# A decoder layer in one kernel: values times output weights ahead of the attention product, which becomes three passes, and the last expert's down weights split one turn earlier

## The chip, the cores and the metric

The kernel runs on one core of one Trainium2 chip. The metric is the device time of one execution in microseconds (us). Engines are named as in the profile: PE is TensorE (matrix products), PEld its weight loads, DVE is VectorE, ACT is ScalarE, POOL is GpSimd, SP is SyncE, which here only issues DMAs.

## The reference

One decoder layer over 1024 tokens of width 1024, all float32: a mixing stage (gated recurrence beside a state-space model, with an output product), then cross-attention into 256 memory tokens, then a mixture of 32 experts with the top 4 for each token, and a final norm. What the change touches:

```python
q = (xn @ xa_wq).reshape(bsz, s, XA_HEADS, XA_HD)            # 4 heads of 256
kv = (rmsnorm(mem, mem_g) @ xa_wkv).reshape(bsz, m, 2, XA_HEADS, XA_HD)
k, v = kv[:, :, 0], kv[:, :, 1]
scores = jnp.einsum('bshd,bmhd->bhsm', q, k) * (XA_HD ** -0.5)
p = jax.nn.softmax(scores, axis=-1)
o = jnp.einsum('bhsm,bmhd->bshd', p, v).reshape(bsz, s, D_MODEL)
return o @ xa_wo
...
gu = xb @ w_gu + b_gu                                          # each expert, on its tokens
h = (u + 1.0) * (g * jax.nn.sigmoid(SWIGLU_ALPHA * g))       # g, u clamped halves of gu
return h @ w_down + b_down
```

## The kernel before

Each engine has its own program, written out by hand; semaphores order them. PSUM has eight banks, and in everything ahead of the experts a list `order` of units sets which bank a unit gets (its number modulo 8): `begin(u)` makes PE wait until the unit eight places earlier has been read out, `end(u)` tells the others that the bank is filled. The order of `order` is therefore PE's order of work.

**Attention.** `q` (in the tensor YT) and the keys (KT) and values (VV, written as units `vv`) are there. A unit `sc` is the scores of 128 tokens against 256 memory tokens for two heads: four float32 products of 256 columns. DVE takes the maxima (`maxima`, L1731), ACT the exponentials with their sums (L1256), DVE divides (`normalise`, L1737 and L1440), and PE transposes the result in a unit `pt` five steps (`LEAD`) after its scores (L846); ACT copies it to PT (L1246). There are 16 of each. Then 16 units `ot` multiply the values with PT, two float32 products of 512 columns each (L856), and ACT copies them to YT (L1052). Then for each of eight row tiles two units `wo2` (`out_tile`, L863) multiply the result with the output weights, eight float32 products each. DVE adds them to H (L1751), PE transposes the new rows (`xt3`) and multiplies them with the router's weights (`rl`, L881), and DVE picks the top 4 (`top`), while DMAs carry the rows out for the experts.

**Two ways to multiply.** A float32 product shows as two records of PE. Where a product is made in three passes (`passes`, L785; the query product L825; all of the experts), ACT rounds an operand to a shorter form (fp32r, the high part), DVE subtracts it from the original (the low part), and PE adds high x high, low x high and high x low; each such product is one record.

**Experts.** A loop of at most 64 turns in groups of four runs over items, of one tile of 128 tokens or two tiles (up to 192) of one expert; a group is skipped once no item is live, and here 36 items are. In turn i PE makes gate and up of item i (L959, L963), then the down product of item i-1 (L980, L987), and the transposes of the next tokens and of the hidden rows (L1012). SP loads raw weights, ACT makes their high parts (`gate_up_high`, `down_high` L1325, `next_high` L1341) and DVE the low parts (L1890, into WL). The last item's down product thus falls into a turn without an item of its own: there `down_pair` on ACT and `down_low` on DVE split its four parts. Tests such as `by_tiles(act, n_i, first)` are branches that each engine runs for itself in every turn. After the loop the tail adds y_acc (L591 loads it) to a bias product (L1036, L1040), normalises and stores. ACT's first work there is L1420.

## Time and profile before

| | |
|---|---|
| median of 3 runs (lowest to highest) | 2292.22 us (2286.15 to 2293.78) |
| the profiled execution: its time, its span | 2293.89 us, 2292.2 us |
| PE busy | 2187.8 us, 95% of the span |
| DVE busy, ACT busy | 1599.9 us (70%), 1271.1 us (55%) |
| moved by DMA | 555.95 MB, mean 243 GB/s |
| mean granted TensorE clock | 0.977 of full speed |

The profile is of one execution. Times of rows count from the start of its span. A row of the timeline merges like instructions in a row (x48 is 48 of them); what stands in brackets behind it is the idle time before it on its engine, and what ended that. PE's records overlap a little, so the step from one row to the next is a better duration than the row's own length.

### The profile page before, as it was taken

The numbers are of one execution on the slowest core, as the hardware profiler recorded it, in microseconds if no ns is written. First come the engines' busy times: TensorE is split into PE (matmuls) and PEld (weight loads), VectorE is DVE, ScalarE is ACT, GpSimd is POOL, SyncE is SP. The second block draws the span as 40 slices with busy tenths as digits, with TensorE's granted clock in tenths as the row PEclk, the third lists the DMA queues.
The fourth block names the chain that finished last, engine by engine and source line by source line (L and its number), as shares of the span: only waits on it lengthen the run. The fifth ranks groups of instructions, "written<-read, shape, count | busy, mean of one in ns | idle before, by whom it ended". The sixth has DMA issues, their size and how long they took to land.

```text
span 2292.2 us, 32993 instructions
## 1 busy us (share of the span) xinstructions
PE 2187.8 (95%) x9450; PEld 1663.6 (73%) x9451; DVE 1599.9 (70%) x1540; ACT 1271.1 (55%) x1209; POOL 459.4 (20%) x357
## 2 busy tenths in 40 slices
PE   7999999999998699999999999999999999999986
PEld 4455668887454588887887888788878887888873
DVE  5645842404134889887779977997889779997773
ACT  3136241415213477666667756776677667776663
POOL 0791000000000113122213212221322123132210
PEclk9999999999998799999999999999999999999997
DMA  5103331111123499989799979999899799997984
GB/s 171 37 1 112 111 146 38 37 37 37 58 96 134 165 378 384 343 305 324 259 320 375 375 275 338 356 361 337 320 316 376 274 323 374 378 379 272 322 294 161
DMA packets 233715, 555.95 MB, mean 243 GB/s; under 512 B 19972, under 2 KB 20200, under 8 KB 232200
## 3 DMA queue, kind: packets, MB, share of 16 engines
q1 hardware_dynamic: 218448, 512.41, 61.0%
q0 software_dynamic: 13264, 42.63, 7.5%
q10 hardware_dynamic: 1960, 0.35, 0.1%
q8 instruction: 26, 0.43, 0.1%
q14 instruction: 17, 0.14, 0.0%
HBM read 518.38 MB, written 33.69 MB: 241 GB/s over the span
## 4 chain that ended last, share of the span: by engine, by line
PE 82%; DVE 7%; issue 6%; ACT 3%; DVEq 1%; ACTq 1%; DMA 0%
PE PS L959 22%; PE PS L627 20%; PE PS L963 12%; PE PS L980 9%; PE PS L987 5%; PE PS L785 4%; PE PS L825 4%; DVE WL L1890 3%; PE PS L951 2%; PE PS L1012 1%; PE PS L917 1%; PE PS L645 1%; PE PS L1040 1%; ACT WH L1320 1%; ACT WH L1325 1%
## 5 line engine op out<-in xcount | busy, mean ns | idle before, releaser
L1890 DVE TENSOR_TENSOR WL<-WA,WH 128x2048 fp32r<-128x2048 f32 x288 | 651.6, 2285 | 70.3 <-ACT WH L1341 46.6
L1890 DVE TENSOR_TENSOR WL<-H,WH 128x2048 fp32r<-128x2048 f32 x144 | 329.2, 2286 | 82.5 <-ACT WH L1320 60.2
L959 PE MATMUL PS<-WH,XEH 128*128 128x512 f32 x1344 | 362.9, 392 | 0.0
L963 PE MATMUL PS<-WL,XEH 128*128 128x512 f32 x1344 | 352.5, 390 | 0.0
L1341 ACT CAST WH<-WA 128x2048 fp32r<-128x2048 f32 x140 | 267.3, 1910 | 144.7 <-PE PS L987 143.2
L959 PE MATMUL PS<-WH,XEL 128*128 128x512 f32 x1152 | 311.5, 393 | 0.0
L963 PEld LDWEIGHTS PS<-WL,XEH 128*128 128x128 f32 x1344 | 253.6, 189 | 53.2
L959 PEld LDWEIGHTS PS<-WH,XEH 128*128 128x128 f32 x1344 | 254.0, 189 | 51.4
L959 PEld LDWEIGHTS PS<-WH,XEL 128*128 128x128 f32 x1152 | 218.6, 190 | 46.4
L980 PE MATMUL PS<-WH,HTH 128*128 128x512 f32 x672 | 187.9, 401 | 6.3 <-DVE WL L1890 6.3
L1320 ACT CAST WH<-H 128x2048 fp32r<-128x2048 f32 x72 | 136.9, 1909 | 86.8 <-PE PS L963 86.6
L1325 ACT CAST WH<-WA 128x2048 fp32r<-128x2048 f32 x72 | 137.5, 1911 | 76.5 <-PE PS L963 75.8
L987 PE MATMUL PS<-WL,HTH 128*128 128x512 f32 x672 | 176.8, 391 | 0.0
L2182 POOL CAST SELR<-WA 128x128 fp32r x35 | 31.0, 885 | 713.1 <-PE PS L917 713.1
L1320 ACT CAST WH<-WA 128x2048 fp32r<-128x2048 f32 x72 | 136.7, 1908 | 36.6 <-PE PS L963 36.6
L1325 ACT CAST WH<-H 128x2048 fp32r<-128x2048 f32 x72 | 136.6, 1907 | 35.1 <-PE PS L963 33.1
L980 PE MATMUL PS<-WH,HTL 128*128 128x512 f32 x576 | 155.4, 392 | 0.0
L987 PEld LDWEIGHTS PS<-WL,HTH 128*128 128x128 f32 x672 | 126.7, 189 | 26.8
L980 PEld LDWEIGHTS PS<-WH,HTH 128*128 128x128 f32 x672 | 121.8, 190 | 28.3 <-DVE WL L1890 6.5
L627 PE MATMUL PS<-XT,WB 128*128 128x512 f32 (+1 forms) x384 | 138.5, 521 | 1.6 <-DVE XT L1464 1.6
L2198 POOL DMA_INDIRECT y_acc<-WA x42 | 90.9, 2164 | 245.2 <-ACT WA L1393 156.1
L980 PEld LDWEIGHTS PS<-WH,HTL 128*128 128x128 f32 x576 | 108.7, 189 | 23.9
(322 smaller groups left out, 2891.2 us busy)
## 6 DMA issues: line engine op xcount, KB each, us to landing
WA<-in_exp_w_gu SPq DMA_DIRECT2D x216, 1024.0 KB, 7.6
H<-in_exp_w_gu SPq DMA_DIRECT2D x72, 1024.0 KB, 7.0
WA<-in_exp_w_down SPq DMA_DIRECT2D x72, 1024.0 KB, 9.5
H<-in_exp_w_down SPq DMA_DIRECT2D x72, 1024.0 KB, 8.3
WB<-in_xa_wkv SPq DMA_DIRECT2D x4, 2048.0 KB, 8.4
WB<-in_w_in SPq DMA_DIRECT2D x3, 2048.0 KB, 9.6
y_acc<-H SPq DMA_DIRECT2D x9, 512.0 KB, 2.6
H<-in_x SPq DMA_DIRECT2D x4, 1024.0 KB, 5.9
```

What stands on the lines that cost most here:

```text
L627: return nc.tensor.matmul(o, a, b, start=(k == 0), stop=(k == n - 1))
L785: ins = nc.tensor.matmul(o, x(k), w(k), start=k_first and n == 0, stop=k_last and n == 3 * len(ks) - 1)
L825: ins = nc.tensor.matmul(o, w[:, k, j * P:(j + 1) * P], x[:, :, k, :], start=n == 0, stop=n == 3 * K - 1)
L959: nc.tensor.matmul(PS[:, 2 * h + t, :], x[:, KT4 * half + k, t * P:(t + 1) * P], WH[:, j % 4, k * HALF:(k + 1) * HALF], start=False, stop= ...
L963: ins = nc.tensor.matmul(PS[:, 2 * h + t, :], XEH[:, KT4 * half + k, t * P:(t + 1) * P], WL[:, j % 4, k * HALF:(k + 1) * HALF], start=Fals ...
L980: nc.tensor.matmul(PS[:, 4 + 2 * t + c, :], hx[:, 2 * m + k, t * P:(t + 1) * P], WH[:, m, k * D + c * HALF:k * D + (c + 1) * HALF], start= ...
L987: ins = nc.tensor.matmul(PS[:, 4 + 2 * t + c, :], HTH[:, 2 * m + k, t * P:(t + 1) * P], WL[:, m, k * D + c * HALF:k * D + (c + 1) * HALF], ...
L1320: nc.scalar.copy(WH[:, s, :], raw_gu(4 + s)).then_inc(gu_high, 1)
L1325: nc.scalar.copy(WH[:, m, :], raw_dn(m)).then_inc(dn_high, 1)
L1341: nc.scalar.copy(WH[:, s, :], raw_gu(s)).then_inc(gu_high, 1)
L1890: v.tensor_tensor(WL[:, s, :], src, WH[:, s, :].bitcast(F32), sub).then_inc(done, 1)
L2198: g.indirect_dma_start(out=y_acc[:, :], out_offset=bass.IndirectOffsetOnAxis(ap=IDS[0:n, t, 0:1], axis=0), in_=YS[0:n, t, :], in_offset=No ...
```

## The change

Two rewrites at once. In attention, `vv` becomes `vt` (the values transposed), and 16 units `vw` multiply each head's values with that head's rows of the output weights, among the score steps; `ot` is gone. `sc` now runs over the first two heads of all tiles, then the other two. ACT rounds `pt` and `vw` to their high parts (`high`), DVE subtracts (`low_part`), and `out_tile` makes 24 products in three passes. In the experts, ACT's and DVE's branches on the number of tiles are merged (`down_pair`, `gate(1)` and `hidden(1)` move into `first`), and the last item's down weights are split in its own turn (`last_high`, `last_low`). The loads of y_acc are cut into 1, 1, 3 and 3 row tiles where they were 2 each.

```diff
-        VV = wa(10240, MT, D)
+        VT = wa(10240, K, ML)
         KV = WA[:, 8192:12288]
-        PP = wa(0, 4, 2, ML)
-        PT = XT[:, :, :].rearrange("p k t -> p (k t)").rearrange("p (h m t) -> p h m t", h=NH, m=MT)
+        PP = wa(12288, 4, 2, ML)
+        PTL = XTR[:, :].rearrange("p (k l s) -> p l k s", l=L, k=K)
+        PTH = WAR[:, 0:8192].rearrange("p (l k s) -> p l k s", l=L, k=K)
...
-        att = [(l, hp) for l in range(L) for hp in range(2)]
-        LEAD = 5
-        for n in range(len(att) + LEAD):
+        att = [(l, hp) for hp in range(2) for l in range(L)]
+        vws = [(c, h, m) for c in range(2) for h in range(NH) for m in range(MT)]
+        LEAD = 4
+        steps_at = []
+        for n in range(L + len(vws)):
             if n < len(att):
-                order.append(("sc",) + att[n])
-            if n >= LEAD:
-                order.append(("pt",) + att[n - LEAD])
-        order += [("ot", h, d, f) for h in range(NH) for d in range(2) for f in range(2)]
+                steps_at.append(("sc",) + att[n])
+            if LEAD <= n < len(att) + LEAD:
+                steps_at.append(("pt",) + att[n - LEAD])
+            if n >= L:
+                steps_at.append(("vw",) + vws[n - L])
+        order += steps_at
+        high_after = [[] for _ in att]
+        for n in range(L + len(vws)):
+            here = high_after[min(n, len(att) - 1)]
+            if LEAD <= n < len(att) + LEAD:
+                here.append(("pt",) + att[n - LEAD])
+            if n >= L and (n - L) % MT == MT - 1:
+                here += [("vw",) + vws[n - L - 1], ("vw",) + vws[n - L]]
+        high_no = {u: n + 1 for n, u in enumerate(sum(high_after, []))}
         for n in range(L + 1):
             order += [("wo2", 0, n)] * (n < L)
...
-                        for n in range(4):
-                            sp.dma_start(ACC[:, 2 * n:2 * n + 2, :],
-                                         y_acc[0:T, :].rearrange("(p l) d -> p l d", l=L)[:, 2 * n:2 * n + 2, :]) \
+                        for n, (l0, l1) in enumerate(acc_part):
+                            sp.dma_start(ACC[:, l0:l1, :],
+                                         y_acc[0:T, :].rearrange("(p l) d -> p l d", l=L)[:, l0:l1, :]) \
                                 .then_inc(acc_in[n], 16)
...
-            for n in range(len(att) + LEAD):
-                if n < len(att):
-                    l, hp = att[n]
-                    o = begin(("sc", l, hp))
+            w_o2 = []
+            for kind, *u in steps_at:
+                o = begin((kind, *u))
+                if kind == "sc":
+                    l, hp = u
...
-                    end(("sc", l, hp), ins)
-                if n >= LEAD:
-                    l, hp = att[n - LEAD]
-                    pe.wait_ge(pn_done, n - LEAD + 1)
-                    o = begin(("pt", l, hp))
+                elif kind == "pt":
+                    n = att.index(tuple(u))
+                    pe.wait_ge(pn_done, n + 1)
...
                         for m in range(MT):
                             ins = nc.tensor.transpose(o[:, (2 * hh + m) * P:(2 * hh + m + 1) * P],
-                                                      PP[:, (n - LEAD) % 4, hh, m * P:(m + 1) * P], ident[:])
-                    end(("pt", l, hp), ins)
-            units_read(pe, "pt")
-            for h in range(NH):
-                for d in range(2):
-                    for f in range(2):
-                        o = begin(("ot", h, d, f))
+                                                      PP[:, n % 4, hh, m * P:(m + 1) * P], ident[:])
+                else:
+                    c, h, m = u
+                    if h == 0 and m == 0:
+                        w_o2.append(weights(("o2", c)))
+                    for d in range(2):
+                        ins = mm(o, VT[:, 2 * h + d, m * P:(m + 1) * P], w_o2[c][:, 2 * h + d, :], d, 2)
+                end((kind, *u), ins)
+            def out_tile(c, n):
+                for hp in range(2):
+                    unit_read(pe, ("pt", n, hp))
+                if n == 0:
+                    for h in range(NH):
                         for m in range(MT):
-                            c = h * HD + d * P
-                            ins = mm(o, VV[:, m, c:c + P], PT[:, h, m, f * HALF:(f + 1) * HALF], m, MT)
-                        end(("ot", h, d, f), ins)
-            units_read(pe, "ot")
-            w_o2 = [weights(("o2", c)) for c in range(2)]
-            def out_tile(c, n):
+                            unit_read(pe, ("vw", c, h, m))
                 o = begin(("wo2", c, n))
-                for k in range(K):
-                    ins = mm(o, YT[:, k, n * P:(n + 1) * P], w_o2[c][:, k, :], k, K)
+                w = WBR[:, chunk_no[("o2", c)] % 2, :, :]
+                i = 0
+                for p_t, m_v in ((PTH[:, n], w), (PTL[:, n], w), (PTH[:, n], MVL[:, c])):
+                    for k in range(K):
+                        ins = mm(o, p_t[:, k, :], m_v[:, k, :], i, 3 * K)
+                        i += 1
                 end(("wo2", c, n), ins)
...
-            def keep(n):
-                l, hp = att[n]
-                u = ("pt", l, hp)
+            def high(u):
                 wait_filled(act, u)
-                evac(act, nc.scalar.copy(PT[:, 2 * hp:2 * hp + 2, :, l * P:(l + 1) * P],
-                                         bank(u).rearrange("p (h m t) -> p h m t", h=2, m=MT)), u)
+                if u[0] == "pt":
+                    _, l, hp = u
+                    o = PTH[:, l, 4 * hp:4 * hp + 4, :]
+                    nc.scalar.copy(o, bank(u).rearrange("p (k s) -> p k s", k=4)).then_inc(att_high, 1)
+                else:
+                    _, c, h, m = u
+                    wait_filled(act, ("vw", c, h, MT - 1))
+                    nc.scalar.copy(WBR[:, chunk_no[("o2", c)] % 2, 2 * h + m, :], bank(u)).then_inc(att_high, 1)
...
-                if n >= LEAD:
-                    keep(n - LEAD)
-            for n in range(len(att) - LEAD, len(att)):
-                keep(n)
-            for h in range(NH):
-                for d in range(2):
-                    for f in range(2):
-                        copy_unit(("ot", h, d, f), YT[:, 2 * h + d, f * HALF:(f + 1) * HALF])
+                for u in high_after[n]:
+                    high(u)
...
                 def down_pair(m0):
                     with act.If_cmp(n_p, 0, "IS_GT"):
-                        with act.If_cmp(n_i, 0, "IS_GT"):
-                            for m in (m0, m0 + 1):
-                                act.wait_ge(gu_used, 8 * i + m + 9)
-                                down_high(m)
-                        with act.Else():
-                            down_high(m0)
-                            down_high(m0 + 1)
+                        for m in (m0, m0 + 1):
+                            act.wait_ge(gu_used, 8 * i + m + 9)
+                            down_high(m)
+
+                def last_high(m):
+                    act.wait_ge(rd_in[m], 16 * i + 16)
+                    act.wait_ge(gu_used, 8 * i + m + 9)
+                    act.wait_ge(dn_used, 4 * i + m + 5)
+                    nc.scalar.copy(WH[:, m, :], raw_dn(m)).then_inc(dn_high, 1)
...
+                    down_pair(0)
+                    gate(1, tiles)
+                    down_pair(2)
+                    if tiles == 2:
+                        upper_up(1)
...
-                by_tiles(act, n_i, first)
-                down_pair(0)
-                by_tiles(act, n_i, lambda tiles: gate(1, tiles))
-                down_pair(2)
-                with act.If_cmp(n_i, P, "IS_GT"):
-                    upper_up(1)
-                counts.fetch(i)
-                by_tiles(act, n_n, next_tokens(0))
-                with act.If_cmp(n_n, 0, "IS_GT"):
+                def tokens_and_weights(tiles):
+                    next_tokens(0)(tiles)
                     next_high(0)
                     next_high(1)
-                by_tiles(act, n_n, next_tokens(1))
+                    next_tokens(1)(tiles)
+
+                def last_weights(m0):
+                    with act.If_cmp(n_i, 0, "IS_GT"):
+                        last_high(m0)
+                        last_high(m0 + 1)
+
+                by_tiles(act, n_i, first)
+                counts.fetch(i)
+                by_tiles(act, n_n, tokens_and_weights, lambda: last_weights(0))
                 by_tiles(act, n_i, hidden(0))
                 with act.If_cmp(n_n, 0, "IS_GT"):
                     next_high(2)
                     next_high(3)
+                with act.Else():
+                    last_weights(2)
                 by_tiles(act, n_i, hidden(1))
                 by_tiles(act, n_p, keep_y)
...
 
+            def low_part(u):
+                dve.wait_ge(att_high, high_no[u])
+                if u[0] == "pt":
+                    _, l, hp = u
+                    ks = slice(4 * hp, 4 * hp + 4)
+                    evac(dve, v.tensor_tensor(PTL[:, l, ks, :], bank(u).rearrange("p (k s) -> p k s", k=4),
+                                              PTH[:, l, ks, :].bitcast(F32), sub), u)
+                else:
+                    _, c, h, m = u
+                    hi = WBR[:, chunk_no[("o2", c)] % 2, 2 * h + m, :].bitcast(F32)
+                    evac(dve, v.tensor_tensor(MVL[:, c, 2 * h + m, :], bank(u), hi, sub), u)
+
             for n in range(len(att) + 1):
                 if n < len(att):
                     maxima(n)
                 if n > 0:
                     normalise(n - 1)
+                    for u in high_after[n - 1]:
+                        low_part(u)
...
+                    with dve.If_cmp(n_p, 0, "IS_GT"):
+                        down_low(0)
+                    gate_min(1, tiles)
+                    with dve.If_cmp(n_p, 0, "IS_GT"):
+                        down_low(1)
+                        down_low(2)
+                    hidden(1, tiles)
+
+                def last_low(m0):
+                    with dve.If_cmp(n_i, 0, "IS_GT"):
+                        for m in (m0, m0 + 1):
+                            dve.wait_ge(dn_high, 4 * i + m + 5)
+                            low_weights(m, raw_dn(m), dn_low)
...
-                with dve.If_cmp(n_p, 0, "IS_GT"):
-                    down_low(0)
-                by_tiles(dve, n_i, lambda tiles: gate_min(1, tiles))
-                with dve.If_cmp(n_p, 0, "IS_GT"):
-                    down_low(1)
-                    down_low(2)
-                by_tiles(dve, n_i, lambda tiles: hidden(1, tiles))
                 counts.fetch(i)
                 by_tiles(dve, n_n, next_tokens(0), lambda: dve.sem_inc(xel_done, 1))
                 with dve.If_cmp(n_p, 0, "IS_GT"):
-                    down_low(3)
-                with dve.If_cmp(n_n, 0, "IS_GT"):
+                    with dve.If_cmp(n_i, 0, "IS_GT"):
+                        down_low(3)
+
+                def weights_and_tokens(tiles):
                     gate_up_low(8)
                     gate_up_low(9)
-                by_tiles(dve, n_n, next_tokens(1), lambda: dve.sem_inc(xel_done, 1))
+                    next_tokens(1)(tiles)
+
+                def no_tokens():
+                    last_low(0)
+                    dve.sem_inc(xel_done, 1)
+
+                by_tiles(dve, n_n, weights_and_tokens, no_tokens)
                 by_tiles(dve, n_i, low_hidden(0))
                 with dve.If_cmp(n_n, 0, "IS_GT"):
                     gate_up_low(10)
                     gate_up_low(11)
+                with dve.Else():
+                    last_low(2)
                 by_tiles(dve, n_i, low_hidden(1))
```

How the instructions move. On PE, the end of attention; L627 is `mm` (L643 in the changed kernel), L846 (L861) are the transposes of `pt`, and products out of XT and WA are `ot`, out of WB and YT `wo2`. Before:

```order
L627 MATMUL PS<-WA,YT 128x256 x4
L846 MATMUL PS<-ident,WA 128x128 x4
L627 MATMUL PS<-WA,YT 128x256 x4
L846 MATMUL PS<-ident,WA 128x128 x24
L627 MATMUL PS<-XT,WA 128x512 x32
L627 MATMUL PS<-WB,YT 128x512 x24
L645 MATMUL PS<-ident,H 128x128 x8
L627 MATMUL PS<-WB,YT 128x512 x8
```

In the changed kernel, at the same place (products out of WB and WA are `vw`; those out of WBR or YTR with WAR or XTR are the three passes of `wo2`):

```order
L861 MATMUL PS<-ident,WA 128x128 x4
L643 MATMUL PS<-WB,WA 128x512 x2
L861 MATMUL PS<-ident,WA 128x128 x4
L643 MATMUL PS<-WB,WA 128x512 x10
L643 MATMUL PS<-WBR,WAR 128x512 x8
L643 MATMUL PS<-WBR,XTR 128x512 x8
L643 MATMUL PS<-YTR,WAR 128x512 x8
```

The block of 32 products has become pairs between the transposes and scores, and a `wo2` unit of eight products has become three times eight.

On DVE, one step of attention: the maxima, their scaling, the reciprocal and the division. Before:

```order
L1731 TENSOR_REDUCE sm<-PS 128x2
L1443 TENSOR_SCALAR sm<-sm 128x2
L1737 RECIPROCAL sm<-sm 128x2
L1440 TENSOR_TENSOR WA<-WA,sm 128x512
L1731 TENSOR_REDUCE sm<-PS 128x2
```

In the changed kernel, a step in the second half of the scores:

```order
L1761 TENSOR_REDUCE sm<-PS 128x2
L1473 TENSOR_SCALAR sm<-sm 128x2
L1767 RECIPROCAL sm<-sm 128x2
L1470 TENSOR_TENSOR WA<-WA,sm 128x512
L1775 TENSOR_TENSOR XTR<-PS,WAR 128x4x128
L1780 TENSOR_TENSOR YTR<-PS,WBR 128x512 x2
L1761 TENSOR_REDUCE sm<-PS 128x2
```

One subtraction for `pt` and, in every other step, two for `vw` have come behind the division.

On ACT, the last part of a turn of the expert loop, from the branch for the other parts of the weights (L1413 before) to the copy of the hidden rows' second half. Before:

```order
L1413 COMPARE_AND_BRANCH
L1338 ISA
L1339 ISA
L1340 ISA
L1341 CAST WH<-WA 128x2048
L1339 REGISTER_ALU
L1340 REGISTER_ALU
L1341 CAST WH<-WA 128x2048
L1413 UNCONDITIONAL_BRANCH
L431 COMPARE_AND_BRANCH
```

In the changed kernel, what has come between that part (which ends with the first row) and the hidden rows:

```order
L1441 UNCONDITIONAL_BRANCH
L1433 COMPARE_AND_BRANCH
L1353 ISA
L1354 ISA
L1355 ISA
L1356 CAST WH<-H 128x2048
L1354 REGISTER_ALU
L1355 REGISTER_ALU
L1356 CAST WH<-H 128x2048
L1433 UNCONDITIONAL_BRANCH
L447 COMPARE_AND_BRANCH
```

The two casts of the last item's down weights stand ahead of `hidden(1)` on ACT.

## Rows read from the trace of the kernel before

**Rows 1.** The page: the chain that ended last, by engine and by line

```profile
PE 82%; DVE 7%; issue 6%; ACT 3%; DVEq 1%; ACTq 1%; DMA 0%
PE PS L959 22%; PE PS L627 20%; PE PS L963 12%; PE PS L980 9%; PE PS L987 5%; PE PS L785 4%; PE PS L825 4%; DVE WL L1890 3%; PE PS L951 2%; PE PS L1012 1%; PE PS L917 1%; PE PS L645 1%; PE PS L1040 1%; ACT WH L1320 1%; ACT WH L1325 1%
```

**Rows 2.** Stretch of the loop: length, busy PE, PEld, DVE, ACT, POOL, clock, DMA share, GB/s

```profile
800.00:2190.00 1390.00, 1369.44 (x6272) 1124.45 (x6272) 1173.31 (x838) 954.98 (x718) 328.14 (x219) 1.00 0.95 336
```

**Rows 3.** Timeline of PE, attention to the first output tiles: start, length, line

```profile
525.09 10.60 PE L627 MATMUL PS<-WA,YT 128*128 128x256 f32 x48 [0.93 <-issue]
...
551.12 1.89 PE L627 MATMUL PS<-WA,YT 128*128 128x256 f32 x8
...
553.29 1.89 PE L627 MATMUL PS<-WA,YT 128*128 128x256 f32 x8
...
564.35 29.40 PE L627 MATMUL PS<-XT,WA 128*128 128x512 f32 x64 [1.71 <-ACT XT L1246]
...
594.69 20.84 PE L627 MATMUL PS<-WB,YT 128*128 128x512 f32 x48 [0.93 <-issue]
```

**Rows 4.** Stretches of the scores, of `ot`, and of `wo2`: columns as in rows 2

```profile
525.00:563.00 38.00, 35.31 (x192) 30.78 (x192) 28.53 (x65) 28.08 (x80) 0.00 (x0) 1.00 0.16 56
563.00:594.00 31.00, 29.40 (x64) 12.67 (x64) 0.00 (x0) 10.04 (x19) 0.00 (x0) 0.94 0.00 1
...
637.00:728.00 91.00, 91.00 (x319) 48.67 (x317) 24.23 (x62) 14.11 (x28) 0.00 (x0) 1.00 0.33 116
```

**Rows 5.** The subtraction of a low part out of PSUM, ns min/median/max

```profile
L1686 DVE TENSOR_TENSOR WAR<-PS,XTR x10: 691/692/693, 432.4 to 440.0; 128x512 fp32r<-128x512 f32 x10
```

**Rows 6.** The chain in order of time: query product; two turns of wo2

```profile
435.61 88.55 PE PS L825 x384
...
637.89 15.52 PE PS L627 x48
654.29 15.52 PE PS L627 x48
```

**Rows 7.** Timeline of PE, keys (256 columns) and values (512 columns)

```profile
237.04 27.86 PE L627 MATMUL PS<-XT,WB 128*128 128x256 f32 x128 [1.64 <-DVE XT L1464]
264.74 27.63 PE L627 MATMUL PS<-WB,XT 128*128 128x512 f32 x64
```

**Rows 8.** Timeline of PE at the router's first product

```profile
624.73 2.45 PE L627 MATMUL PS<-WA,XT 128*128 128x32 f32 x16 [1.46 <-DVE WA L1440]
626.99 10.03 PE L627 MATMUL PS<-WB,YT 128*128 128x512 f32 x16
```

**Rows 9.** Timeline of all engines, end of the last item and last down product

```profile
2220.20 2.29 DVE L1890 TENSOR_TENSOR WL<-H,WH 128x2048 fp32r<-128x2048 f32 x1 [0.33 <-issue]
...
2227.91 0.60 PE L1012 MATMUL PS<-ident,WA 128*128 128x128 f32 x4
...
2234.79 2.07 PE L980 MATMUL PS<-WH,HTH 128*128 128x512 f32 x4 [6.29 <-DVE WL L1890]
...
2248.85 1.11 ACT L1393 ACTIVATE WA<-PS,WA 128x1024 f32<-128x1024 f32 x1 [11.03 <-PE PS L987]
```

**Rows 10.** Down weights' loads (L540) after 2200 us: us from issue to landing

```profile
DMA to landing us min/median/max: 4.8/5.1/7.6
```

**Rows 11.** The chain after the last product: ACT's queue in its empty turns

```profile
2249.98 0.04 ACTq L1404
...
2252.78 0.04 ACTq L1404
...
2253.10 0.96 ACTq L452
...
2256.58 0.28 ACTq L452
...
2261.69 1.05 ACT HTH L1420
```

**Rows 12.** PE's longest wait in the expert loop: us, times, longest

```profile
PE PS L1012 <- DVE XEL L1886: 13.7, 13, 4.7
```

30 lines of the change are left out of this document (17 added, 13 removed).

## The prediction

> **What bounds the kernel now.** The page's chain first: PE has 82% of what ended last, the expert products alone nearly half [rows 1]. The stretches confirm it for the expert loop: from 800 to 2190 us PE is busy 1369.4 of 1390 us at full clock, while the DMA engines are busy at 0.95 and DVE at 1173 [rows 2]. So what the change does inside a normal turn of the loop can give back 20.6 us at most, and only a saving of PE work, or of a wait of PE, counts elsewhere. Next the timeline of PE in attention: one step (a score unit and a transpose unit) takes 553.29 - 551.12 = 2.17 us with no idle time, then `ot` starts after a wait of 1.71 for ACT, and the first `wo2` after another 0.93 [rows 3]. Attention, too, is bound by PE, with small waits where one kind of unit ends. The end is different: ahead of the last down product PE waits 6.29 us for the low parts of the weights [rows 9], and from ACT's copy of its result at 2248.85 [rows 9] ACT's queue runs through empty turns until its first work of the tail at 2261.69 [rows 11].
>
> **Values.** `vv` takes 27.63 us of PE (64 records of 512 columns), `kk` 27.86 (128 of 256) [rows 7]. `vt` has the shape and count of `kk`, so it costs +0.2 us at most. The loads behind it wait for its middle and its end, as they did. I take 0.
>
> **Attention.** Removed: 16 `ot` units, and the two waits around them. Added to the score steps: 16 `vw` units of the same shape, two products of 512 columns, four records. A record of 512 columns takes 20.84 / 48 = 0.43 us, so a unit 1.72 [rows 3]. PE's work is then 16 x 2.17 + 16 x 1.72 = 62.2 us, where the stage took 594.69 - 525.09 = 69.6 us [rows 3]: 7.4 us less, if nothing new makes PE wait. What hides beside it: ACT copied each `pt` and each `ot` and rounds each `pt` and `vw` now, 32 of one size as before: 28.08 + 10.04 = 38 us [rows 4]. DVE was busy 28.53 us for 16 steps [rows 4], 1.8 a step, 1.9 with gaps, and gets 32 subtractions of 0.69 [rows 5]: 16 x 1.9 + 32 x 0.69 = 52.5 us. Both are below 62.2. In the dense part, steps 8 to 15, PE needs 3.9 us a step, DVE 1.9 + 2 x 0.69 = 3.3. The wait added on DVE is for ACT's high part; behind it stand the next maxima, then ACT's exponentials, then a `pt` that PE makes four steps later, so there is room. Tightest are the banks: the first `vw` of a pair is only read out once the second is made and rounded, and PE wants its bank eight units later. From the start of a step DVE has it out after 1.7 (scores) + 1.9 (own work) + 2 x 0.69 = 5.0 us, and PE comes to it after 3.9 + 1.7 = 5.6. That fits by 0.6. If it did not, four pairs would each lose about 1 us. Bounds: 2 to 8 us gained; I take 7.4.
>
> **Output product.** Each of 16 `wo2` units was 8 float32 products, 16 records x 0.43 = 6.9 us. It becomes 24 products in three passes. The query product has their shape: 384 of them in 88.55 us, 0.2306 each [rows 6], so 5.53 us. Saved: 16 x 1.37 = 22 us (22.5 by 20.84 / 48 unrounded). The rest of a row tile's turn of 654.29 - 637.89 = 16.4 us (transposes, router) stays [rows 6]. DVE has 24.23 of 91 us in this stage and ACT 14.11 [rows 4], 4.4 and 2.5 a turn, so they don't take over at 13.6. The wait of 1.46 us for the scaled router weights, and the slow products after it (10.03 us for 16 records against 6.9) [rows 8], come again: it hangs on DVE's add and multiply behind the second tile's product, whatever that took. Bounds: 18 (the slow piece grows, or a turn gets a wait of 0.5) to 23; I take 22.
>
> By the rows a float32 product takes 0.86 us and one pass of the other kind 0.2306, a ratio of 3.7 [rows 3, 6]. The Trainium skill, "FP8 and Floating Point Precision", TensorE Precision Notes, has a true FP32 product at 4 passes through the array. By that, a unit would fall by a quarter of 6.9, to 5.2, and the stage by 27 us; the sum goes by the rows.
>
> **The normal turns.** DVE's and ACT's order of work is the same, with fewer branches. PE's longest wait there, 13.7 us in 13 pieces for the low part of the next tokens [rows 12], comes at the end of a run of DVE work without gaps, so branches hardly lengthen it. 0, bounds -4 (slower) to +4.
>
> **The last item.** Now its weights' split stands ahead of the last down product, on queues that run in order. The last load is issued when DVE ends `down_low(3)`, about 2220.20 + 2.29 = 2222.5 [rows 9], and lands after about 5.1 [rows 10], 2227.7. ACT may write a part once PE has used the old one; counted back from 2227.91 [rows 9] in parts of 12 products of 0.23 with one block of transposes between, that is from 2219.5, 2222.2, 2225.4 and 2228.1, the last one to 2230. `hidden(0)` stands ahead of the third, and only after the fourth comes `hidden(1)`. DVE: five subtractions of 2.29 (`down_low(3)` and four) and two of 0.69 from 2220.2 make 12.8, so 2233.1 with PE's signal. PE starts the last down product at 2233.2 in place of 2234.79: the wait of 6.29 shrinks by 1.6 only, since the last low part of the hidden rows now comes after the weights. With a last load of 7.6 [rows 10] the start is 2235.7, 0.9 late. The transposes of the second half wait for parts 0 and 1 on DVE (2227.1), PE comes at 2227.91: covered by 0.8.
>
> **The empty turns.** A turn without work costs ACT 2252.78 - 2249.98 = 2.8 us [rows 11] for 12 tests, 0.23 a test. Eight tests are left, and three such turns follow: 3 x 4 x 0.2 = 2.4. PE leaves the loop by turns of its own, which stay as they were, and is next late; I let 2.2 count. The smaller first loads of y_acc end no wait, since PE wasn't waiting for them. Together the end gives 3.8 us; bounds -1 to 8 (8 if the clock also stays up over the shorter wait).
>
> **Sum.** 7.4 + 22 + 0 + 3.8 = 33 us off the profiled execution's 2293.89: 2261. The median of the runs, 2292.22, is 1.7 lower, so the same saving gives 2259. I say 2260.
>
> **Rivals.**
> 1. As summed: 2260, own range 2254 to 2267. Chance 0.65.
> 2. DVE or the banks hold attention back. For it: a margin of 0.6 us a pair, and DVE loaded to 85%. Against: the counts above. At 1 to 1.5 us for each of four pairs, and 1 to 2 at the hand-over to `wo2`, 6 us are lost: 2266. Chance 0.13.
> 3. The end gains nothing: the order of ACT's queue makes `hidden(1)` late and a slow load eats the rest; the empty turns hit a slow one like the 0.96 against 0.28 of the loop's own read [rows 11]. 4 to 5 us lost: 2264. Chance 0.12.
> 4. Turned over: the longer branch bodies on ACT and DVE cost a jump that has to load code in each turn. For it: that row of 0.96 [rows 11] is a stumble of 0.7 us after a jump back, and the two-tile case now stands as a longer block ahead of the one-tile case. Against: PE is busy 98.5% through 36 items [rows 2], so such stumbles are hidden now. It decides from 33 / 36 = 0.9 us a turn that PE feels; at 1.3 us, 47 are lost: 2306. Chance 0.04. The Trainium skill, "Runtime: NRT & Kernel Launch", Instruction fetch mechanics, says that a taken branch out of the loaded window makes the sequencer fetch the target before it goes on; the 0.7 us would fit, but no row here shows what the longer bodies do.
> 5. More than summed (the clock stays up at the wait before the last product and at the router, the loop gains 4): 2251. Chance 0.06.
>
> **Numbers.** Cases 1, 2, 3 and 5 lie between 2248 and 2272; cut to 8 in 10 the range is 2252 to 2271. About 0.3% (7 us) is what a measurement can tell here. Faster by more than that holds in all but case 4 and its milder form, in which the turns eat about all: 0.95 faster, 0.02 within, 0.03 slower.
>
> **What would show it.** In the changed profile: no `ot` records; PE from the first score to the first `wo2` in 62 to 64 us; a `wo2` unit at 5.5, a row tile's turn at 13.6 to 13.8; PE's wait before the last down product 4.5 to 5 us, ended by DVE's low part of the hidden rows; ACT's empty turns near 2.0; the stretch of the loop still at 98% PE. Wrong would be: a wait of PE on a bank or on DVE among the `vw` units; a turn above 14 us; a lower granted clock from the first `vw` to the router; a longer wait for the next tokens in normal turns.

## The result and the profile after

| | before | changed |
|---|---|---|
| median (lowest to highest, 3 runs each) | 2292.22 us (2286.15 to 2293.78) | 2254.76 us (2253.54 to 2256.15) |
| profiled execution: time, span | 2293.89, 2292.2 us | 2254.76, 2253.0 us |
| PE busy, share of the span | 2187.8 us, 95% | 2156.8 us, 96% |
| mean granted TensorE clock | 0.977 | 0.983 |

The ratio is 0.9842, with a 95% interval of 0.9824 to 0.9861: 37.5 us faster, where 32 (2292 to 2260) were forecast, inside the range of 2252 to 2271. The kernel before ran 65 times in all (median 2289.97 us, 2286.04 to 2294.55), most of them near 2286.5 or near 2293; the median of the three above and both of its profiles are of the upper group, so some 2 of the 37.5 us are the draw. The chain of the changed kernel answers to [rows 1]. PE is still what ended last in four fifths of the span; the page says:

```profile
PE 80%; issue 8%; DVE 6%; ACT 3%; DVEq 1%; ACTq 1%; DMA 1%; SPq 0%
```

Next the timeline of PE from the first score to the router, as [rows 3, 8]:

```profile
525.58 8.87 PE L643 MATMUL PS<-WA,YT 128*128 128x256 f32 x40 [0.98 <-ACT YT L1072]
...
543.39 1.88 PE L643 MATMUL PS<-WB,WA 128*128 128x512 f32 x4
545.11 1.89 PE L643 MATMUL PS<-WA,YT 128*128 128x256 f32 x8
546.83 0.60 PE L861 MATMUL PS<-ident,WA 128*128 128x128 f32 x4
547.27 1.88 PE L643 MATMUL PS<-WB,WA 128*128 128x512 f32 x4
...
579.19 8.75 PE L643 MATMUL PS<-WB,WA 128*128 128x512 f32 x20
587.37 2.42 PE L643 MATMUL PS<-WBR,WAR 128*128 128x512 f32 x8
...
612.47 1.97 PE L643 MATMUL PS<-WA,XT 128*128 128x32 f32 x16 [1.46 <-DVE WA L1470]
614.28 2.10 PE L643 MATMUL PS<-WBR,WAR 128*128 128x512 f32 x8
...
628.03 2.11 PE L643 MATMUL PS<-WBR,WAR 128*128 128x512 f32 x8
```

A dense step is 547.27 - 543.39 = 3.88 us, with no idle time in any row of the units `vw`, and the waits of 1.71 and 0.93 [rows 3] at the change of units are gone. At the router PE waits 1.46 us, as in [rows 8], but what follows runs at full speed: eight products in 616.22 - 614.28 = 1.94 us, where in the kernel before the 16 records of the unit took 10.03 and those of the next one 7.03. A row tile's turn is 628.03 - 614.28 = 13.75 us, where it was 16.4 [rows 6].

The end, in the timelines of PE, ACT and DVE, as [rows 9, 11]:

```profile
2194.19 0.60 PE L1032 MATMUL PS<-ident,WA 128*128 128x128 f32 x4
2194.39 1.90 ACT L1356 CAST WH<-H 128x2048 fp32r<-128x2048 f32 x1 [0.81 <-PE PS L1007]
2196.19 0.58 ACT L1406 CAST HTH<-PS 128x512 fp32r<-128x512 f32 x1
2196.32 2.29 DVE L1934 TENSOR_TENSOR WL<-H,WH 128x2048 fp32r<-128x2048 f32 x1 [0.37 <-ACT WH L1356]
2196.67 1.12 ACT L1419 ACTIVATE WA<-PS,WA 128x1024 f32<-128x1024 f32 x1
2198.53 0.68 DVE L2034 TENSOR_TENSOR HTL<-PS,HTH 128x512 fp32r<-128x512 f32 x1
2199.35 1.46 PE L1000 MATMUL PS<-WH,HTH 128*128 128x512 f32 x4 [4.57 <-DVE HTL L2034]
...
2212.32 1.11 ACT L1419 ACTIVATE WA<-PS,WA 128x1024 f32<-128x1024 f32 x1 [14.53 <-PE PS L1007]
2223.80 1.04 ACT L1450 CAST HTH<-H 96x1024 fp32r<-96x1024 f32 x1 [10.36 <-issue]
```

PE's wait fell from 6.29 to 4.57 us and is now ended by the low part of the hidden rows, behind the last subtraction of the weights.

Cut at the same landmarks, the two profiled executions differ stage by stage. The landmarks on PE are the first score, the first `wo2`, the last transposes of rows for the router, the last transposes (L1012, now L1032) of the first turn and of the last item, the last down product and the last product of the tail; on ACT its last `keep_y` copy and its first work of the tail. Three of before's were not shown yet:

```profile
728.28 1.07 PE L645 MATMUL PS<-ident,H 128*128 128x128 f32 x8
...
800.43 1.11 PE L1012 MATMUL PS<-ident,WA 128*128 128x128 f32 x4 [4.74 <-DVE XEL L1886]
...
2284.12 1.88 PE L1040 MATMUL PS<-WA,ident 128*128 128x512 f32 x4
```

and in the changed kernel they stand at:

```profile
696.83 1.07 PE L661 MATMUL PS<-ident,H 128*128 128x128 f32 x8
...
768.63 1.12 PE L1032 MATMUL PS<-ident,WA 128*128 128x128 f32 x4 [4.77 <-DVE XEL L1930]
...
2245.01 1.88 PE L1060 MATMUL PS<-WA,ident 128*128 128x512 f32 x4
```

| stage (us) | before | changed | difference | forecast |
|---|---|---|---|---|
| up to the first score | 525.09 | 525.58 | +0.5 | 0 |
| attention | 69.60 | 61.79 | -7.8 | -7.4 |
| output products, router | 133.59 | 109.46 | -24.1 | -22 |
| item lists, first turn | 72.15 | 71.80 | -0.35 | 0 |
| loop up to the last item's transposes | 1427.48 | 1425.56 | -1.9 | 0 |
| to the last down product | 6.88 | 5.16 | -1.7 | -1.6 |
| to ACT's copy of it | 14.06 | 12.97 | -1.1 | 0 |
| empty turns, to ACT's tail | 12.84 | 11.48 | -1.4 | -2.2 |
| tail's sums, and from there to the end | 30.5 | 29.2 | -1.3 | 0 |
| sum | | | -39.2 | -33 |

### The profile page after: what moved, and what is told of

Same layout as the page of the kernel before. It is cut to its first block, busy times and chain, and to the rows that moved or that the text cites. A ratio compares the mean times of both kernels' runs of the same rounds, so it can differ in the third digit from the quotient of the medians.

```text
span 2253.0 us, 32880 instructions
## 1 busy us (share of the span) xinstructions
PE 2156.8 (96%) x9642; PEld 1696.1 (75%) x9643; DVE 1620.0 (72%) x1572; ACT 1271.3 (56%) x1213; POOL 453.0 (20%) x357
## 4 chain that ended last, share of the span: by engine, by line
PE 80%; issue 8%; DVE 6%; ACT 3%; DVEq 1%; ACTq 1%; DMA 1%; SPq 0%
PE PS L979 21%; PE PS L643 20%; PE PS L983 11%; PE PS L1000 9%; PE PS L1007 5%; PE PS L801 4%; PE PS L841 4%; DVE WL L1934 2%; PE PS L971 2%; PE PS L1032 1%; ACT WH L1339 1%; PE PS L937 1%; PE PS L661 1%; PE PS L1060 1%; ACT WH L1362 1%
## 5 line engine op out<-in xcount | busy, mean ns | idle before, releaser
L643 PE MATMUL PS<-XT,WB 128*128 128x512 f32 (+1 forms) x512 | 166.2, 486 | 1.6 <-DVE XT L1494 1.6
L1344 ACT CAST WH<-H 128x2048 fp32r<-128x2048 f32 x70 | 132.9, 1907 | 33.5 <-PE PS L983 32.0
L643 PEld LDWEIGHTS PS<-XT,WB 128*128 128x128 f32 x512 | 97.2, 190 | 69.1 <-issue 62.6
```

The lines of the kernel that those rows point to most:

```text
L643: return nc.tensor.matmul(o, a, b, start=(k == 0), stop=(k == n - 1))
L1344: nc.scalar.copy(WH[:, m, :], raw_dn(m)).then_inc(dn_high, 1)
```

## The experiments

Each kernel ran beside the kernel before on the same chip; ratios are to that, with 95% intervals. The stages named are those of the table.

### One part alone

**e_att: the attention part on top of the kernel before.** The edit is the upper part of the diff, from VT to `low_part`.

> The kernel before with the values-times-weights rewrite alone. If the parts simply add on PE's path: attention stage 61.8 us from the first score to the first output product, a row tile's turn 13.76 us, the router's transposes 31 to 32 us earlier than before, and 2258 to 2262 us in all. If the gain of the loop's stretch (1.9 us in the two profiles) belongs to the attention part (other starting times of loads), the first expert's last transposes to the last item's come 1.9 us closer and the time is 2257 to 2259. Rival, part of the 37 us comes only from both together: above 2263.

Measured: 2263.41 us, ratio 0.9884 (0.9866 to 0.9903). The expected 2258 to 2262 us were missed by 1.4. Attention takes 61.79 us and the output stage 109.46, to 0.01 us as in the changed kernel. So these two stages don't need the loop part. The 8.7 us that this profile has more than the changed one lie behind it: loop 1428.42 (+2.9), to the last down product 6.98 (+1.8), to ACT's copy 14.23 (+1.3), empty turns 13.40 (+1.9), tail (+1.1). The rival's bound of 2263 was passed by 0.4 us. It was no good test, since it left out both the loop part's own gain and the pieces at a lower clock that are told under before_again; so the whole times leave the rival open (see e_loop).

**e_loop: the loop part on top of the kernel before**, from `acc_part` and `last_high` on.

> The kernel before with the rewrite of the expert loop's end alone (with the y_acc loads of 1, 1, 3 and 3 row tiles). If the parts add: 4 to 8 us faster than before, 2284 to 2288, with PE's wait ahead of the last down product 4.5 to 4.7 us in place of 6.29 and 11.5 us from ACT's copy of the last result to its first work of the tail in place of 12.84. If the branches help the normal turns, the loop's stretch is 1.5 to 2 us shorter here too. Rival, longer branch bodies cost in each turn: slower than before.

Measured: 2286.35 us (12 runs, 2282.08 to 2290.57) beside 2287.66 (17 runs, 2286.04 to 2294.03), ratio 0.9993 (0.9982 to 1.0003): by the medians not told apart, lowest and highest run 4.0 and 3.5 us lower. The stages show the parts that were expected: to the last down product 5.20 (wait 4.61), empty turns 11.60. Rival 4, a price in each turn, would be 47 us and is refuted. The whole times don't add up: beside the same 17 executions of the kernel before, e_att saves 24.3 us, e_loop 1.3, and both parts (e_acc, below) 33.5. By the profiles e_loop is 8.5 us shorter (span 2283.7 for 2292.2). Where the missing 8 us come from is not shown: 10 of those 17 executions took 2286.0 to 2288.0 us, and no profile of such a one was taken.

**e_acc: y_acc loaded by two row tiles, as before.**

```diff
-        acc_part = ((0, 1), (1, 2), (2, 5), (5, L))
...
+                pe.wait_ge(acc_in[l // 2], 16)
```

> The changed kernel with the y_acc loads of two row tiles each, as before. If PE never waits for them: the same time within 1 us (2255). Rival, the small first loads are what lets the tail's first products start earlier (they start 1.3 us closer to ACT's first work of the tail than before): 1 to 1.5 us slower, with a wait of PE in the tail ended by a load.

Measured: 2254.15 us, ratio 0.9848 (0.9833 to 0.9863), no wait of PE on a load in the tail. The smaller loads are worth nothing here, as forecast.

**e_merge: merged branches, but the last item's weights split one turn later.**

```diff
+                def late_high():
+                    with act.If_cmp(n_p, 0, "IS_GT"):
+                        for m in range(4):
+                            down_high(m)
-                by_tiles(act, n_i, first)
+                by_tiles(act, n_i, first, late_high)
...
-                by_tiles(act, n_n, tokens_and_weights, lambda: last_weights(0))
+                by_tiles(act, n_n, tokens_and_weights)
```

(likewise `late_low` on DVE, in place of `last_low`.)

> The changed kernel with the last item's down weights split in the turn behind it, as before; attention, the merged branches and the y_acc loads stay. If the merged branches alone make the normal turns shorter: 1424 to 1425.6 us from the first item's last transposes to the last item's, as in the changed kernel, where the kernel with the attention part alone has 1428.4; and if the split alone makes the end's wait shorter: PE waits 6.3 us ahead of the last down product again, and 1.7 to 2 us are lost against the changed kernel (2256.5). Rival, the loop's 3 us hang on the split or on when the loop starts: the loop's stretch is 1427 to 1428.5 here as well, and 4 to 5 us are lost.

Measured: 2260.61 us, ratio 0.9876 (0.9854 to 0.9898): 5.9 us above the changed kernel's 2254.76. PE's wait is 6.18 us again, ended by the low part of the weights: the split is what shortened it. But the loop is 1428.43 us, the rival's number, and neither theory explains it. Its PE row at the start of an item, and the same one in the changed kernel:

```profile
878.32 0.49 PE L971 MATMUL PS<-BIASR,SELR 128*128 128x512 f32 x1 [0.56 <-issue]
```

```profile
878.64 0.49 PE L971 MATMUL PS<-BIASR,SELR 128*128 128x512 f32 x1 [0.38 <-issue]
```

PE's own program is the same in both, and what it waits for here the profile doesn't show. In about twenty places of the 35 turns, most of them the start of an item, it comes 0.1 to 0.2 us later, 3.5 us in all with the low-clock pieces of the next section taken off. The edit touches branches on ACT and DVE alone, and it is not a test more in a turn: ACT has one else branch more and two fewer, DVE one more and one fewer. So PE feels how the branches of the other engines lie, in spite of its 98.5%. Whether it is the longer body that is jumped over, its place in the code or its order is not shown.

### Where the loop's difference comes from

**before_again: the kernel before once more.**

> The kernel before, unchanged, as a second profile of it. Its 17 runs beside the last experiments lay in two groups, around 2286.5 and around 2293. If this profile falls in the lower group: its loop from the first item's last transposes to the last item's is near 1424 us in place of 1427.5, or the slow piece at the router is shorter, or both, and so the change's saving over a like execution is 32 to 33 us rather than 37. If the profile lies in the upper group, its stages repeat those of the first one within 1 us.

Measured: 2292.44 us (12 runs), profiled execution 2292.01, again of the upper group, so the expectation for the lower one (a saving of 32 to 33 us) stays untested. Up to ACT's tail every stage of the table is within 0.05 us of the first profile (attention 69.60, output 133.60, loop 1427.46, to the down product 6.88), except the stretch ahead of the first score (1.9 us less). A profile is a good ruler, then. What differs between kernels are short pieces behind a wait of PE in which the granted clock falls to one half (of its two levels, the lower). PE in e_att, timeline:

```profile
1430.58 0.49 PE L970 MATMUL PS<-BIASR,SELR 128*128 128x512 f32 x1 [0.67 <-issue]
1430.92 1.31 PE L978 MATMUL PS<-WH,XEH 128*128 128x512 f32 x4
1432.02 1.91 PE L978 MATMUL PS<-WH,XEL 128*128 128x512 f32 x4
1433.73 1.69 PE L982 MATMUL PS<-WL,XEH 128*128 128x512 f32 x4
```

and in the changed kernel, at the same item and behind the same wait:

```profile
1430.42 0.49 PE L971 MATMUL PS<-BIASR,SELR 128*128 128x512 f32 x1 [0.63 <-issue]
1430.75 1.08 PE L979 MATMUL PS<-WH,XEH 128*128 128x512 f32 x4
1431.67 1.07 PE L979 MATMUL PS<-WH,XEL 128*128 128x512 f32 x4
```

The stretches of 4 us from there have a granted clock of 0.58 and 1.00. One such piece costs 1.7 us. With each row's excess over 1.07 us taken off, the loop is 1422.0 us in the kernel before (5.4 us of excess), 1422.3 in e_att (6.1), 1420.8 in the changed kernel (4.7), 1420.8 in e_loop and e_acc (3.2 each), and 1424.3 in e_merge (4.1). So the loop part gives back 1.2 to 1.5 us of PE's path in 35 turns, and apart from e_merge and e_blocks (told below) the rest of the loop's differences is the clock. Between the two profiles of the kernel before the pieces stand at the same items and add up to the same (5.45 and 5.44 us); e_acc, whose work up to the last item is the changed kernel's, has two in the loop where that has three.

### The attention stage

**e_f32: the output product in one float32 pass.**

```diff
-                for p_t, m_v in ((PTH[:, n], w), (PTL[:, n], w), (PTH[:, n], MVL[:, c])):
-                    for k in range(K):
-                        ins = mm(o, p_t[:, k, :], m_v[:, k, :], i, 3 * K)
+                for k in range(K):
+                    ins = mm(o, PTH[:, n, k, :].bitcast(F32), w[:, k, :].bitcast(F32), k, K)
```

> The changed kernel, but the output product is made once, in float32, from the rounded high parts (the low parts are still made and nobody reads them, so their share of the product is left out). If the two savings of attention are separate ones: 61.8 us from the first score to the first output product, as in the changed kernel, and 16.4 us a row tile's turn, as before, so 2275 to 2279 us in all. If the slow products behind the router's wait came from PE's waits at the end of attention, which are gone here: no piece of 8 to 10 us there. If they come and go with the execution: present or not, whatever stands ahead. Rival, the three passes are what pays for the hiding (float32 products would make PE wait for the units): a wait of PE ahead of the first output product.

Measured, one run: 2276.63 us. Attention 62.19, output 131.84: the two savings are separate. PE at the router, timeline:

```profile
617.23 2.06 PE L643 MATMUL PS<-WA,XT 128*128 128x32 f32 x16 [1.46 <-DVE WA L1467]
619.10 8.74 PE L643 MATMUL PS<-WBR,WAR 128*128 128x512 f32 x16
```

The slow piece is there without any wait at the end of attention, so it doesn't come from those waits: 1.7 us over 7.03, where before had 3.0 and e_loop 1.6. Of the ten profiles with the three passes, eight have none (109.45 to 109.49 us for the stage, the changed kernel's among them), e_twice has 1.6 and e_acc, whose attention is the changed kernel's, 3.2 (112.65). So behind the same 1.46 us it came in all four profiles with a float32 output product and in two of ten with three passes. Whether the kind of product that stands ahead has a part in that, or only the draw, no run here separates. The Trainium skill, "TensorE: Matmul & The Clock Gate", Part 1, says that the number of slow products at the start of one and the same kernel changes from run to run, since the chip's window of activity is not tied to the program; e_acc beside the changed kernel fits that, the two profiles of the kernel before, which agree, don't show it.

**e_twice: each low part of a `vw` unit subtracted twice.**

```diff
+                    v.tensor_tensor(MVL[:, c, 2 * h + m, :], bank(u), hi, sub).then_inc(again, 1)
+                    dve.wait_ge(again, vws.index((c, h, m)) + 1)
```

> The changed kernel with the subtraction of each of the 16 values-times-weights units made twice on DVE, the second after the first. If the banks have a margin of 0.6 us a pair, as worked out ahead of the change: 1.4 to 1.6 us more a pair exceed it, PE waits 0.8 to 1 us for a bank at each of four pairs in the dense part, and attention takes 65 to 66 us in place of 61.8. If the margin is wider (units read out sooner than counted, since PE's eight units are further apart than the step): no wait, 61.8 to 62.5 us, DVE busy 58 us of it. If it is narrower: above 67.

Measured: 2257.56 us, ratio 0.9853 (0.9839 to 0.9866). Attention 63.26 us, 1.5 more than in the changed kernel, in a few small gaps: between the 61.8 to 62.5 expected of a wide margin and the 65 to 66 of one of 0.6. PE's timeline, and the stage's stretch (length, busy PE, PEld, DVE, ACT, POOL, clock, DMA share, GB/s):

```profile
563.22 0.66 PE L861 MATMUL PS<-ident,WA 128*128 128x128 f32 x4 [0.31 <-DVE YTR L1782]
```

```profile
525.60:588.80 63.20, 62.60 (x255) 42.29 (x256) 55.62 (x107) 36.39 (x95) 0.00 (x0) 1.00 0.09 34
```

Four pairs cost PE 0.2 to 0.5 us each. At 1.4 to 1.6 us more DVE work for a pair, the margin is then about 1.1 us (an estimate) and not 0.6. Banks and DVE are what comes next, as rival 2 had it, but not yet. (The other half of the 3 us is a slow piece at the router, 111.07.)

### The end

**e_order: the hidden rows ahead of the last two weight parts.** The same on DVE, with `low_hidden(1)` and `last_low(2)`.

```diff
                 with act.Else():
+                    by_tiles(act, n_i, hidden(1))
                     last_weights(2)
-                by_tiles(act, n_i, hidden(1))
```

> The changed kernel, but in the last item's turn ACT's and DVE's work on the second half of the hidden rows stands ahead of the last two parts of the down weights. If the wait of 4.57 us is made by that order: PE begins the last down product 1.3 to 1.6 us after its transposes in place of 5.2, finds parts 2 and 3 ready (their low parts end 5.4 and 7.7 us after the transposes), and the kernel is 3 to 4 us faster than the changed one (2251). Rival, the weights themselves are late: PE stands still inside the down product ahead of part 2 or 3, and at most 1 us is gained.

Measured: 2257.11 us, ratio 0.9864 (0.9844 to 0.9883): nothing gained (2.3 us above the changed kernel), and for a reason that I had not listed. Its timelines of ACT and PE:

```profile
2194.48 0.58 ACT L1406 CAST HTH<-PS 128x512 fp32r<-128x512 f32 x1 [3.95 <-PE PS L1032]
2194.97 3.70 ACT L1356 CAST WH<-H 128x2048 fp32r<-128x2048 f32 x2
2198.57 1.12 ACT L1419 ACTIVATE WA<-PS,WA 128x1024 f32<-128x1024 f32 x1
...
2199.93 2.07 PE L1000 MATMUL PS<-WH,HTH 128*128 128x512 f32 x4 [5.48 <-ACT WA L1419]
```

The last down product writes the PSUM banks of the one before, and `keep_y`, which reads them out, is last in ACT's queue. In the changed kernel it ends at 2197.8, hidden by the late low part; here both casts stand ahead of it.

**e_order2: `keep_y` and DVE's `add_y` ahead of the last weights as well.**

```diff
                 with act.Else():
                     by_tiles(act, n_i, hidden(1))
+                    by_tiles(act, n_p, keep_y)
                     last_weights(2)
```

> The changed kernel, but in the last item's turn ACT's and DVE's work on the second half of the hidden rows, and the copy of the item before's result out of PSUM (keep_y, add_y), all stand ahead of the last two parts of the down weights. The run e_order left PE waiting 5.48 us for that copy, which had come behind both casts. If the banks of the result were the only other thing in the way: PE waits 1.9 us in place of 4.57, parts 2 and 3 are ready in time, and 2 to 3.5 us are gained against the changed kernel (2251 to 2252). Rival, the copy takes DVE's and ACT's time and the low parts are late inside the product: under 1 us gained. Rival, the longer bodies cost in the normal turns: slower than the changed kernel.

Measured: 2252.88 us (2251.18 to 2253.14), ratio 0.9834 (0.9821 to 0.9848). PE's timeline:

```profile
2191.84 0.60 PE L1032 MATMUL PS<-ident,WA 128*128 128x128 f32 x4
2194.36 1.93 PE L1000 MATMUL PS<-WH,HTH 128*128 128x512 f32 x4 [1.93 <-ACT WA L1419]
```

The wait is 1.93 us as worked out, and no part is late inside the product: 2.6 us less up to the product than in the changed kernel. The tail gives 1.3 of them back (30.5 us for 29.2). The medians are 1.9 us apart (1.3 from e_acc's), and the five runs all lie below the three of the changed kernel (2253.54 to 2256.15), though on another chip.

**e_fill: products that nobody reads, in PE's idle time.**

```diff
+                def no_gate_up():
...
+                            filler(14)
+                    with pe.Else():
+                        filler(8)
-                by_tiles(pe, n_i, gate_up)
+                by_tiles(pe, n_i, gate_up, no_gate_up)
```

> The changed kernel, with products that nobody reads put ahead of the last down product (14 of 512 columns) and into the empty turns (8 each), into a bank that nothing uses then. If the slow products behind PE's waits come from its having been idle: the last down product runs at full clock (11.0 us to ACT's copy in place of 13.0 to 14.2), the first tail products too (1.5 to 2 us less), 3 to 4 us gained in all (2251). Rival, the idle time isn't what lowers the clock, or the products delay PE's leaving of the loop: the same slow rows, or the transposes behind the loop later, 2255 to 2260.

Measured: 2253.70 us, ratio 0.9834 (0.9819 to 0.9850). PE's timeline:

```profile
2193.53 3.47 PE L1038 MATMUL PS<-BIASR,SELR 128*128 128x512 f32 x14
2198.35 1.19 PE L1000 MATMUL PS<-WH,HTH 128*128 128x512 f32 x4 [1.35 <-DVE HTL L2047]
...
2226.33 3.56 PE L1073 MATMUL PS<-WA,ident 128*128 128x512 f32 x4
```

The 3 us behind 2198.4 have a granted clock of 1.00, those behind 2199.4 in the changed kernel 0.62: what lowered the clock there was PE's idle time. Behind e_order2's shorter wait of 1.93 us it is low too (0.52 from 2194.4 to 2197.4). The clock was worth 1.6 us on PE (10.10 us from the product's first row to its last, for 11.71). Of that 1.2 arrive, 11.74 us to ACT's copy in place of 12.97, since ACT now waits for a load of POOL's, as in e_best below. The tail's first products stay slow (3.56 us), and PE still idles 4.93 and 2.81 us ahead of them; with 3.06 and 2.10 in e_best their granted clock is still 0.57, so that this idle time is the cause is not shown. The expected 2251 us was not reached: the median is 1.1 below the changed kernel's and not told apart from it.

**e_blocks: the groups of turns in blocks of four.**

```diff
+            with eng.Fori(0, GROUPS // 4) as a:
+                with eng.If_cmp(counts.live, 0, "IS_GT"):
+                    with eng.Fori(0, 4) as b:
```

> The changed kernel with the loop's 17 groups of turns taken in blocks of four, a block being skipped as a whole once no item is live, where each of the groups left over costs ACT 0.58 us now. ACT's way from its copy of the last result to its first work of the tail is 11.5 us; six groups are skipped in the changed kernel, two groups and one or two blocks here: 1.2 to 1.7 us less, so 2253 in place of 2254.5, as far as PE's transposes, which end at the same time, come earlier too. Rival, the extra level costs ACT or PE a stumble of 0.7 us each time it is passed: no gain.

Measured: 2254.26 us, ratio 0.9837 (0.9823 to 0.9851), the same as the changed kernel. ACT's way to the tail shrank to 10.03 us, as expected (0.58 of it because this loop has 16 groups and not 17, which is enough for the 36 items here), and was given back in the turns: first turn +0.5, PE's wait 4.93 in place of 4.57, and the loop without the slow pieces 1424.1 us, 3.3 more. The new test is passed once in sixteen turns; what each turn has more is the reckoning of its number from three counters in place of two. Which part of the edit the 3.3 us are is not shown.

**e_best: e_order2, e_blocks and the unread products together**, 6 ahead of the down product, 8 in each empty turn, 8 in the tail.

> The changed kernel with all that helped so far: the copy of the item before's result and the second half of the hidden rows ahead of the last weights (order2), 6 unread products ahead of the last down product and 8 in each empty turn, 8 more behind the transposes of the tail, and the groups in blocks of four. If these add: wait 1.9 and part of it filled, 11.7 us from the last down product to ACT's copy in place of 13.0, 10 us to the tail in place of 11.5, and the first products of the tail at full clock, 1 to 1.5 us: 2247 to 2249 in all. Rival, the unread products are late themselves in PE's order and push what follows: 2251 to 2253, as order2 alone.

Measured: 2251.66 us (2248.37 to 2255.75), ratio 0.9832 (0.9816 to 0.9847): beside e_order2 no difference that counts. PE ended the product 11.1 us after its start, but ACT's copy came 13.31 after it. The chain there:

```profile
2194.55 6.39 DMA y_acc<-WA
...
2204.77 2.42 DMA WA<-gate_rows,WA
...
2207.30 0.06 ACT WA L1435
```

POOL stores the item before's rows (6.39 us), and only then fetches the gates that scale the last copy. In the changed kernel POOL issued the same fetch at 2208.60, so that by 2.4 to 2.6 us a fetch it ended about 1 us ahead of PE's product. In e_order2 (2204.66) the two end together: the chain is the bound as soon as PE is faster, and e_fill's copy already waited for it. The version to keep is e_order2, which has about the same time with the smallest edit.

## Why the prediction was right

**Values.** Keys' shape and count for `vt`, 0. Right: from the first product of the keys to the end of `vt` PE takes 292.71 - 237.39 = 55.32 us, where it took 292.21 - 237.04 = 55.17. The stretch up to the first score is +0.5 us, within the 1.9 us by which the two profiles of the kernel before differ there.

**Attention, -7.4.** Right: 61.79 us where 62.2 was worked out, steps of 3.88 us for 3.9. The count of DVE (52.5 us) was high: 47.38 us in the 62. The bank margin of 0.6 us was too small by half a microsecond (e_twice), on the safe side.

**Output product, -22.** The price was right: a row tile's turn is 13.75 us. The sum was mis-sized in one term: "the slow products after it come again". They didn't, which gave 3.0 of the 24.1 us; the rest, some 8 x 2.64 = 21.1, is the product's. The piece came in e_acc and e_twice and in no other profile with the three passes, so how much of the 3 us is the rewrite's and how much this execution's stays open.

**Normal turns, 0.** The bound of 4 held. On PE's path they gave 1.2 us; the reason given, that branches stand behind DVE work without gaps, is only partly right, since e_merge and e_blocks lose 3.3 to 3.5 us though no engine is given other work in a turn.

**The last item, -1.6.** Right in place, releaser and size (4.57 us, ended by L2034). What I had not seen is the second wait just behind it, on `keep_y`; without it e_order would have looked like a sure gain.

**Empty turns, -2.2.** The mechanism was right, the size was off: 2.26 us a turn and not 2.0, so -1.4. The chain of the changed kernel, from turn to turn, the stumble, and two skipped groups:

```profile
2214.78 0.04 ACTq L481
...
2217.04 0.04 ACTq L481
...
2217.72 0.99 ACTq L468
...
2220.75 0.04 ACTq L479
...
2221.33 0.04 ACTq L479
```

A test left out saves less than the 0.2 us that I took: (2.8 - 2.26) / 4 = 0.14 us. One of the turns stumbles by 0.7 us in both kernels.

**Sum.** By like pieces the change is worth 7.8 + 21.1 + 0.35 + 1.2 + 1.7 + 1.4 = 33.5 us less the 0.5 ahead of it, 33, what was forecast. The 6 us on top are low-clock pieces that before's profile has and the changed one lacks: 3.0 at the router, 0.7 in the loop, 1.1 behind the last wait, 1.3 in the tail. e_fill shows for the third of these that idle time of PE makes it; the others are read from the rows only. That the time fell inside the range was thus the sum's doing, and that it fell 5 us below 2260 these pieces' and the draw's: by the median of all 65 executions of the kernel before the change is worth 35 us, and e_acc, which lacks only the smaller loads, gains 33.5 over the 17 beside it.

## What to carry to other kernels

Work that is put among other units costs PE only its own products if the engines that read it out have room; count the bank's way (filled, rounded, subtracted, wanted again), and double the suspected step to measure the margin. Before moving work forward in a queue, list every wait of the consumer, not only the last one: the next one may be an earlier result that stands at the end of the same queue. And compare kernels stage by stage at fixed landmarks, with the low-clock pieces taken off, before a difference of 2 or 3 us is put down to an edit.

## What the hardware showed that was not expected

- The same wait (0.63 to 0.67 us behind one of 0.98) is followed by a piece at half clock in one kernel (e_att) and not in another whose normal turns differ only in their branches (the changed one); a piece costs 1.7 us, and 1.0 to 6.1 us of them lie in a loop of some 1425 us.
- How branches and loop levels are laid out reaches PE at 98.5% busy: 0.1 to 0.2 us in many turns, 3.3 to 3.5 us over 35 (e_merge, e_blocks), with no test more in a normal turn.
- 14 products that nobody reads, put into a wait of PE, kept the granted clock at 1.00 where it was 0.62, worth 1.6 us on PE (e_fill).
- A loop of groups that are skipped isn't free: in the changed kernel a skipped group takes ACT's queue 0.58 us, and the seven that are skipped behind the last item (the expectation of e_blocks says six) 3.8 of the 11.48 us.
